# Replacing the barrier between input projection and middle stage by waits for single producers, in a two-layer hybrid decoder step

## The reference

```
z = rmsnorm(x) @ w_in        # 3264 columns: q_r k_r v_r g_r | q_lat c_raw kpe_raw | g_a
q_r, k_r = rope(q_r), rope(k_r) / sqrt(dk);  o_r = groupnorm(retention(q_r, k_r, v_r)) * silu(g_r)
q = rmsnorm(q_lat) @ w_qb;  qn = rmsnorm(q[:128]);  qp = rope(rmsnorm(q[128:]))   # per head
c = rmsnorm(c_raw);  kpe = rope(rmsnorm(kpe_raw))
kn = rmsnorm(c @ w_kb);  v = c @ w_vb
o_a = softmax(qn.kn + qp.kpe) @ v * silu(g_a)   # new sequences also attend to 2048 cached rows each
x = x + concat[o_r, o_a] @ w_out
```

## Time and profile before

| | us |
|---|---|
| median of 3 runs (lowest, highest) | 1260.67 (1259.77, 1263.28) |
| the profiled execution's own time | 1260.41 |
| its span, first to last instruction | 1258.6 |
| PE busy in the span | 1220.8 |
| DVE, ACT, POOL busy | 725.8, 527.4, 436.8 |

### The profile page before, as it was taken

How to read it: one execution, slowest core, us unless ns; L and a number is a source line. 1 busy time by engine, 2 the same in 40 slices (tenths; PEclk the granted TensorE clock), 3 DMA queues, 4 the chain that set the end, 5 groups by cost and what they waited for, 6 DMA issues and landing times.

```text
span 1258.6 us, 26097 instructions
## 1 busy us (share of the span) xinstructions
PE 1220.8 (97%) x8624; PEld 1126.8 (90%) x8624; DVE 725.8 (58%) x1322; ACT 527.4 (42%) x1377; POOL 436.8 (35%) x632
## 2 busy tenths in 40 slices
PE   5999999998999999999999999999989999999998
PEld 4999995767999999999999999767779999999998
DVE  5445646665666666666463474556546666666652
ACT  4221324534655555553341122353446555555520
POOL 1014035441544454541011220554324544454400
PEclk9999999999999999999999999999999999999999
DMA  9331104102462232220743130320044433222021
GB/s 319 109 106 55 54 1 107 52 1 73 142 188 74 79 83 80 74 57 7 251 131 108 54 107 1 89 70 1 15 142 143 128 85 84 74 74 82 23 70 51
DMA packets 127906, 108.41 MB, mean 86 GB/s; under 512 B 45682, under 2 KB 123635, under 8 KB 127795
## 3 DMA queue, kind: packets, MB, share of 16 engines
q1 hardware_dynamic: 127794, 107.08, 28.4%
HBM read 96.12 MB, written 10.91 MB: 85 GB/s over the span
## 4 chain that ended last, share of the span: by engine, by line
PE 83%; issue 7%; DVE 3%; POOL 2%; ACT 2%; POOLq 1%; DVEq 1%; DMA 0%; ACTq 0%
PE ps L977 30%; PE ps L562 7%; PE ps L563 7%; PE ps L564 7%; PE ps L954 5%; PE ps L648 3%; PE ps L1006 3%; PE ps L572 2%; PE ps L573 2%; PE ps L986 2%; PE ps L804 1%; PE ps L827 1%; POOL rstat L2166 1%; PE ps L805 1%; PE ps L661 1%
## 5 line engine op out<-in xcount | busy, mean ns | idle before, releaser
L2000 DVE TENSOR_REDUCE kss<-ksq 128x8 f32<-128x1024 f32 x128 | 156.0, 1219 | 180.2 <-ACT ksq L1486 180.2
L562 PE MATMUL ps<-w_hi,hT_hi 128*128 128x408 f32 (+2 forms) x704 | 242.9, 345 | 0.0
L1486 ACT ACTIVATE ksq<-ps 128x544 f32<-128x544 f32 x256 | 159.9, 625 | 195.9 <-PE ps L977 195.3
L563 PE MATMUL ps<-w_lo,hT_hi 128*128 128x408 f32 (+2 forms) x704 | 239.9, 341 | 0.0
L564 PE MATMUL ps<-w_hi,hT_lo 128*128 128x408 f32 (+2 forms) x704 | 239.3, 340 | 0.0
L977 PE MATMUL ps<-wq_hi,cT_hi 128*128 128x272 f32 x1024 | 224.3, 300 | 0.0
L2336 POOL TENSOR_TENSOR krs<-kss_t,cst 128x8 f32<-128x8 f32 x128 | 209.2, 1634 | 19.0 <-issue 2.6
L977 PE MATMUL ps<-wq_lo,cT_hi 128*128 128x272 f32 x1024 | 212.4, 289 | 0.0
L977 PE MATMUL ps<-wq_hi,cT_lo 128*128 128x272 f32 x1024 | 212.4, 289 | 0.0
L977 PEld LDWEIGHTS ps<-wq_lo,cT_hi 128*128 128x128 f32 x1024 | 161.5, 189 | 0.0
L977 PEld LDWEIGHTS ps<-wq_hi,cT_lo 128*128 128x128 f32 x1024 | 161.3, 189 | 0.0
(11 more groups left out here) (202 smaller groups left out, 1996.2 us busy)
## 6 DMA issues: line engine op xcount, KB each, us to landing
ckv<-in_cache_ckv SPq DMA_DIRECT2D x256, 128.0 KB, 2.0
raw<-in_w_in SPq DMA_DIRECT2D x64, 408.0 KB, 4.4
kp<-in_cache_kpe SPq DMA_DIRECT2D x256, 32.0 KB, 1.8
S<-in_state_ret SPq DMA_DIRECT2D x8, 512.0 KB, 6.0
out<-S SPq DMA_DIRECT2D x8, 512.0 KB, 3.2
wout<-in_w_out SPq DMA_DIRECT2D x8, 344.0 KB, 4.5
z<-in_w_out SPq DMA_DIRECT2D x8, 340.0 KB, 10.2
raw<-in_w_out SPq DMA_DIRECT2D x8, 340.0 KB, 4.5
```

The costliest lines, as they stand in the source:

```text
L562: pe.matmul(out, a_hi, b_hi, start=first, stop=False)
L563: pe.matmul(out, a_hi, b_lo, start=False, stop=False)
L1486: act.activation(ksq[:, q % 2, j, :].rearrange("p (s c) -> p s c", s=2), ps[:, 1 + 2 * j:3 + 2 * j, 0:CUT], ACT.Square).then_inc(kk_sq, 1)
L2000: dve.tensor_reduce(kss[:, hs, 2 * k:2 * k + 2, :], ksq[:, q % 2, :, c0:c0 + HW].rearrange("p j (h k) -> p j h k", h=H), AX.X, ALU.add).th ...
```

## The change

The first of the two barriers goes, the one between input projection and middle stage. In its place stand waits on single counters, DVE keeps the tiles of group 7 between the latents of the next tiles, the transposed `w_kb` goes to banks 3 and 4, and ACT does `tanh(0)` and `tanh(1)` behind `keep_latents(0)` and `keep_wkbT`.

```diff
--- before.py
+++ after.py
@@ -381,11 +381,11 @@
     X_OUTS = 6
     SMALL = 10
 
-    def stage_end(eng, L, k):
+    def stage_end(eng, L):
 
         eng.drain()
         eng.sem_inc(stage, 1)
-        eng.wait_ge(stage, len(engines) * (2 * L + k + 1))
+        eng.wait_ge(stage, len(engines) * (L + 1))
 
     block_cm = nc.Block()
     block = block_cm.__enter__()
@@ -451,7 +451,7 @@
                     sp.dma_start(raw[:, k, :, :], w_in_t[L][:, 2 * k:2 * k + 2, g * GW:(g + 1) * GW])\
                         .then_inc(raw_in[k], 16)
 
-            sp.wait_ge(stage, 4 * (2 * L + 1))
+            sp.wait_ge(z_in_psum, NG * TILES)
             for h in range(H):
                 sp.dma_start(S0[:, h, :, :], state_ret[L:L + 1, :, h, :, :]
                              .rearrange("l b k e -> k (l b) e")).then_inc(s0_in, 16)
@@ -500,7 +500,7 @@
             sp.wait_ge(s_ok, S_TILE)
             sp.dma_start(ret_p[L:L + 1, 0, :, :, :].rearrange("l h k e -> k (l h) e"),
                          S[:, :, :]).then_inc(state_out, 16)
-            sp.wait_ge(stage, 4 * (2 * L + 2))
+            sp.wait_ge(stage, 4 * (L + 1))
             sp.wait_ge(state_out, 16 * (L + 1))
             for k in range(4):
                 sp.dma_start(wout0[:, k, :, :], w_out_t[L][:, 2 * k:2 * k + 2, 0:N0]).then_inc(wout0_in, 16)
@@ -615,15 +615,17 @@
                 pe.wait_ge(w_lo_ok, N_W * L + g * 4 + 4)
                 for t in range(TILES):
                     tile_product(g, t)
-            stage_end(pe, L, 0)
 
 
             def latents(t):
                 n = rows(t)
-                pe.wait_ge(lat_ok, t + 1)
+                pe.wait_ge(lat_ok, TILES)
                 if t >= 1:
 
                     pe.wait_ge(q_ok, t)
+                else:
+
+                    pe.wait_ge(z_kept, (NG - 1) * TILES + 1)
                 for c in range(KC):
                     pe.transpose(ps[:, 0, c * P:c * P + n], zc(t, C_C + c * P, P), ident[0:n, 0:n])
                 pe.transpose(ps[0:ROPE, 0, KC * P:KC * P + n], kpe[0:n, t, :], ident[0:n, 0:n])
@@ -635,6 +637,8 @@
                 pe.wait_ge(lat_kept, 3 * (t + 1))
                 if t >= 1:
                     pe.wait_ge(qp_kept, t)
+                else:
+                    pe.wait_ge(z_kept, (NG - 1) * TILES + 2)
                 for c in range(KC):
                     m = pe.matmul(ps[:, 2, :], cT[:, t % 2, c, :], wvb[:, c, :], start=c == 0, stop=c == KC - 1)
                 m.then_inc(v_ps, 1)
@@ -689,10 +693,11 @@
                 m.then_inc(qp_turned, 1)
 
             def turn_wkb():
+                pe.wait_ge(z_kept, (NG - 1) * TILES + S_TILE)
                 for h in range(H):
                     for c in range(KC):
                         n = h * KC + c
-                        m = pe.transpose(ps[:, 6 + n // 4, (n % 4) * P:(n % 4 + 1) * P],
+                        m = pe.transpose(ps[:, 3 + n // 4, (n % 4) * P:(n % 4 + 1) * P],
                                          wkb[:, c, h * DK:(h + 1) * DK], ident)
                 m.then_inc(wkbT_ps, 1)
 
@@ -721,7 +726,8 @@
                 t = mix_tile(k)
                 n = rows(t)
                 if k == 0:
-                    pe.wait_ge(wkbT_kept, 1)
+                    pe.wait_ge(z_kept, NG * TILES)
+                    pe.wait_ge(roped, TILES)
                 else:
 
                     pe.wait_ge(up_ok, H)
@@ -793,6 +799,7 @@
                 i, h = divmod(n, H)
                 if n == 0:
                     pe.wait_ge(pads_ok, 1)
+                    pe.wait_ge(wkbT_kept, 1)
                 if h == 0:
                     pe.wait_ge(q_kept, i + 1)
                     pe.wait_ge(qp_kept, i + 1)
@@ -933,7 +940,7 @@
             attend(14)
             turn_probs(15)
             attend(15)
-            stage_end(pe, L, 1)
+            stage_end(pe, L)
             S1 = L * NB
 
 
@@ -1250,17 +1257,17 @@
                                    accum_out=stat[0:n, k * 8 + t:k * 8 + t + 1]).then_inc(lat_sq, 1)
                 act.drain()
             move_z(NG - 1)
-            stage_end(act, L, 0)
 
 
             def keep_wkbT():
                 act.wait_ge(wkbT_ps, 1)
                 act.activation(wkbT[:, :, :].rearrange("p h (c k) -> p (h c k)", c=KC),
-                               ps[:, 6:8, :].rearrange("p b n -> p (b n)"), ACT.Copy).then_inc(wkbT_kept, 1)
+                               ps[:, 3:5, :].rearrange("p b n -> p (b n)"), ACT.Copy).then_inc(wkbT_kept, 1)
 
             def tanh(t):
 
                 n = rows(t)
+                act.wait_ge(z_kept, (NG - 1) * TILES + t + 1)
                 if t >= 2:
                     act.wait_ge(gate_ok, t - 1)
                 act.activation(gate[0:n, t % 2, :], zc(t, C_GA, HW), ACT.Tanh, scale=0.5).then_inc(gate_tanh, 1)
@@ -1377,10 +1384,10 @@
                 act.activation(prT[:, n % 2, 0:(i + 1) * P], ps[:, 5, 0:(i + 1) * P], ACT.Copy).then_inc(pT_kept, 1)
 
             act.wait_ge(qkn_ok, 1)
+            keep_latents(0)
+            keep_wkbT()
             tanh(0)
             tanh(1)
-            keep_latents(0)
-            keep_wkbT()
             tanh(2)
             tanh(3)
             tanh(S_TILE)
@@ -1459,7 +1466,7 @@
             keep_probs(14)
             probs(15)
             keep_probs(15)
-            stage_end(act, L, 1)
+            stage_end(act, L)
             S1 = L * NB
 
 
@@ -1600,8 +1607,8 @@
             def keep_x_lo(t):
                 keep_lo(t, X_BANKS, x_turned, x_hi, 0, x_lo, 1.0)
 
-            def keep_z(g):
-                for t in range(TILES):
+            def keep_z(g, tiles=range(TILES)):
+                for t in tiles:
                     n = rows(t)
                     dve.wait_ge(z_in_psum, TILES * g + t + 1)
                     dst = z[0:n, t, g * GW:(g + 1) * GW]
@@ -1726,10 +1733,11 @@
                 dve.sem_inc(lat_ok, 1)
 
 
-            for t in range(TILES):
+            latents(0)
+            for t in range(1, TILES):
                 latents(t)
-            keep_z(NG - 1)
-            stage_end(dve, L, 0)
+                keep_z(NG - 1, (t - 1,))
+            keep_z(NG - 1, (S_TILE,))
 
 
             def sum_q(t):
@@ -1966,7 +1974,7 @@
             new_scores_out()
             attn_out(14)
             attn_out(15)
-            stage_end(dve, L, 1)
+            stage_end(dve, L)
             S1 = L * NB
 
 
@@ -2209,7 +2217,8 @@
                     inv_root(rstat[:, c], stat[:, c], pool_tmp[:, c], 1, 1.0 / w, EPS, None)
                 pool.drain()
                 pool.sem_inc(lat_rs, 1)
-            stage_end(pool, L, 0)
+
+            pool.wait_ge(z_in_psum, NG * TILES)
 
             def qp_root(t):
                 n = rows(t)
@@ -2312,7 +2321,7 @@
             ret_root(S_TILE)
             ret_y(S_TILE)
             pool.wait_ge(out_done, 16 * OUTS * (L + 1))
-            stage_end(pool, L, 1)
+            stage_end(pool, L)
             S1 = L * NB
```

## The result

The changed kernel took 1254.08 us, median of 4 runs (1252.22 to 1255.54), against 1260.26 for the kernel before on the same chip. The ratio is 0.9942 with a 95% interval from 0.9925 to 0.9959, so 7.3 us; the two medians themselves differ by 6.2, a ratio of 0.9951, which lies in the interval. Two later sets of runs gave 0.9938 (0.9924 to 0.9951) and 0.9939 (0.9926 to 0.9952). The forecast was 1254.7. The profiled execution took 1253.29, with a span of 1251.4 (before: 1260.41 and 1258.6).

A forecast was written before the change was run, and what follows sets the result against it. TensorE (PE), with 83% of the chain, was taken to bound the kernel. Gains of 4.6 + 0.2 + 0.2 + 1.04 = 6.0 us took the profiled 1260.41 to 1254.4, and the median to 1254.7; range 1252.9 to 1257.8.

The forecast's parts named there:

- The gap: Projection to middle stage: PE's wait at the barrier goes, gaining 2.29 (layer 0) and 2.49 (layer 1), less 0.2: 4.6 us.
- ACT's order: Middle stage start: with `tanh` behind ACT's copies, `q_project(0)` starts about 1.9 behind the first transpose, gaining 0.2 a layer.
- The copies and POOL: Between the `latents`: DVE's PSUM copies were taken to slow POOL's roots by nothing, at most 0.58, a whole copy.
- The clock: Layer 1, first transpose to end of `q_project(0)`: without the gap no fall to 1.2 GHz, 7.23 becomes 6.19, gaining 1.04.
- Downstream: Behind the middle stage's start: the gain passes through whole; the decode junctions' clock may move the time 1.5 either way.
- The sum: Whole kernel: 4.6 + 0.2 + 0.2 + 1.04 = 6.0 us gained, so a median of 1254.7.
- Late latents: Rival, end of projection: the copies hold up POOL's roots or DVE, giving 1255.9 to 1257.7; chance 0.12.
- Clock not back: Rival: gap closed, but the low clock stays in layer 1 or moves elsewhere, giving 1255.7 or 1257.2; chance 0.15.
- Gain eaten later: Rival: the middle stage ends on something unmoved, or short waits of ACT and DVE grow, giving 1260.7; chance 0.08.
- The gates as a new bound: Rival, middle stage: `tanh` and `gates` rounds over 1.45 delay ACT and PE; at 1.9 a round, 1265; chance 0.03.

## Why the prediction was right

**The gap.** It was said to shrink from 2.48 and 2.68 to 0.19 plus 0.1 for waits, 4.6 in all. It shrank to 0.18: 2.30 + 2.50 = 4.8. The 0.1 of waits isn't there. The last `latents` came early enough: counted as the prediction did, the slack was 0.35 in both layers, where it had read 0.34 and 0.14. The run with the copies behind all `latents` shows what happens without the holes.

**ACT's order.** `q_project(0)` was put 1.9 behind the first transpose and came at 1.88 and 1.89. The worth of 0.2 per layer was right in the sum (2.12 became 1.88), since it compares the new order with the order of before behind a barrier. But the run with ACT's order of before shows that without the barrier the order is worth 0.86 per layer. The prediction did not say so: a change that moved the copies and took the barrier away, but left ACT as it was, would have gained 0.86 less a layer.

**The copies and POOL.** No root grew. The holes in layer 1 were 1.25 in three places and 1.56 in the fourth, so the three copies of 0.58 had room. The Trainium skill, SBUF — State Buffer, "Who interferes with whom", says that an operation with at most one SBUF input outside the two-port modes doesn't contend with GpSimd, and the rows agree: 0.55 beside the copy from PSUM. For a copy from SBUF, which by that section can hold the pair, the roots took 0.58 and 0.61: the cost is there, at 0.03 to 0.06.

**The clock.** The step said that the low stretch belonged to the gap but did not follow each one, and took 1.04 for layer 1. In the pair of profiled executions that was right: 7.23 became 5.95 there, 1.04 of it by clock. For the medians this term was too small: with 3 of 4 places it is 1.6 in all, since layer 0 pays it as well at times, which one profile couldn't show, and the decode junctions add to it. The granted clock that each execution has on record says the same. Among the profiled executions it is 0.999 where none of the places counted above has a low stretch, 0.997 or 0.998 with one, 0.996 with two, 0.994 with three. The executions of the kernel before have 0.9940 and 0.9941 on average in the two later sets, those of the changed kernel 0.9970 and 0.9988: about two and three low stretches fewer.

**Downstream.** The stretches from `ret_turn(0)` to the last `attend` are equal to 0.01, so the gain passed through whole. The junctions to the decode stage moved by 1.5 each, in opposite directions, as the range allowed.

**The sum.** 6.0 forecast; 6.32 in the change's own place in the two profiles, of which waits and order are 5.3 and the clock 1.04. By the ratios of the three sets the change gives 7.3 to 7.8, with intervals from 5 to 9.5; 5.3 and the average 1.6 for the clock make 6.9, which lies inside. With about two and three low stretches fewer, by the granted clocks, at 0.7 to 1.5 each (see below), it would be 6.7 to 8.3 and 7.4 to 9.8 in the two later sets, against 7.8 and 7.7. So waits and order were forecast within 0.3 (5.0 against 5.3). That the median came within 0.6 of the forecast is in part luck, since the clock's share was too small for the medians, and the stretches at the decode junctions, 1.5 each, could have moved it further.

**The rivals.** Late latents: no, by the roots. Clock not back: no, in none of 20 places, and the granted clocks above say that the low stretches became fewer and did not just move. Gain eaten later: no. The gates as a new bound: not reached, by 0.9 of cover, which the prediction had worked out as 1.16 - 0.5 = 0.7. Its threshold was of the right kind: the run with every `tanh` twice passed the cover by 1.5 and lost 1.7 a layer.

**What stays open.** The kernel with the barrier kept and only the copies moved gained 6.4 and 4.8, where its waits and the clock behind its own gaps account for 3.4. Its profiled executions don't show why, since they were the slowest of their sets (1261.49 among others of 1255.36 to 1256.24, and 1258.42 among 1254.97 to 1256.83). The first one has a low stretch at a decode junction (9.18 to the first L986 instead of 7.63), a wait for cached pages with a low stretch behind it (1.70 and 1.5), and a late start:

```profile
986.07 1.11 PE L954 MATMUL ps<-cst,ckv 128*128 128x128 f32 x4 [1.70 <-DMA ckv<-in_cache_ckv]
```

But the granted clocks of the others are on record: 0.999 to 1.000 in the first set and 0.998 or 0.999 in the second, so none or one of the low stretches, while the kernel before beside them had 0.993 in six of nine executions, and 0.9958 on average in the second set. That makes about three and two low stretches fewer. What one costs the whole time is less sure: 1.04 to 1.5 in the timelines, but near 0.7 by the executions of the kernel before (19 in one set: the median is 1262.2 at a clock of 0.993 and 1260.1 at 0.997, some three stretches apart). With 0.7 to 1.5 each, and 1.8 for the waits, this kernel should gain 3.9 to 6.3 and 3.2 to 4.8, against the measured 6.4 and 4.8: both intervals overlap with it. Why the shorter first gap goes with fewer low stretches at the decode junctions 110 us later isn't shown. Nor is what makes PE wait for the cached pages in some executions. The start of the kernel, where the first products run slowly, also differs by up to 1.6 between profiles (188.31 to 189.90 for the last product of layer 0), without a link to the edits.

## What to carry to other kernels

A barrier costs at least what the slowest engine has queued in front of it, so before removing one, move that queue into the idle holes ahead: here four copies, and this alone brought PE's first transpose from 2.5 or 2.7 behind its last product to 1.7. Then look at what each engine does first behind the barrier, since an order that cost little while everybody waited (two `tanh` ahead of the copies PE needs, 0.24 a layer) becomes the next wait (0.86). And read the clock behind each gap in more than one profile, and the granted clock of the executions without one: here a gap of 2.33 cost 1.04 more through the slower stretch that followed it.

## What was not expected of the hardware

DVE's copy of 64x256 from SBUF to SBUF in `clear()`, and POOL's memsets beside it, in layer 0. Before:

```profile
192.73 1.07 DVE L1879 COPY c_new<-z 64x256 f32<-64x256 f32 x1
...
192.71 0.95 POOL L2274 MEMSET qpT<- 64x1024 f32 x1
```

After:

```profile
190.79 0.42 DVE L1887 COPY c_new<-z 64x256 f32<-64x256 f32 x1
...
190.50 0.57 POOL L2284 MEMSET kpeT<- 64x576 f32 x1
```

The copy took 1.07 before and 0.42 after. Both times it started while a memset of POOL ran, and both times it ended 0.14 behind the memset's end (193.80 and 193.66; 191.21 and 191.07). It is so in all 28 places of the fourteen profiles, 0.14 or 0.15 behind the end of what POOL had running: with the copies behind all `latents` that is its mask product, and the copy takes 0.80; in the first run with the barrier kept it is, in layer 0, a second memset right behind the first, and the copy takes 1.59. So here VectorE stood until GpSimd was done. The Trainium skill, SBUF — State Buffer, "Who interferes with whom", says that, where a VectorE instruction uses both ports, the one that is issued first gets the shared pair for its whole instruction and the other is blocked; for the memset the trace agrees, for the root in the run with the extra SBUF copies (0.58 and 0.61 beside 0.55, the copy at 0.37) it shows nearly nothing of it. An operation's length in one profile can thus be another engine's, and moves when the order does. The copy lay off the critical path here.
